# Fetching norm weight rows two norms ahead, and summing two halves of an attention output in one operation, in a two-block transformer kernel

## The reference, cut to what matters

```python
def group_layernorm(x, g):                 # used for each gMLP group and each retention head
    mu = mean(x); var = mean((x - mu)**2)
    return (x - mu) * rsqrt(var + EPS) * g # g: 128 weights for each group or head

outs.append(einsum('bhqk,bkhe->bqhe', attn, vb))   # both attentions: probabilities times values
```

## Time and profile before

| what | value |
|---|---|
| median of 3 runs | 4096.31 us (4092.6 to 4104.3) |
| profiled execution, its own time | 4091.48 us |
| span of its trace | 4089.7 us |
| busy PE, DVE, ACT, POOL | 3780.2, 2004.9, 1698.1, 798.5 us |
| mean TensorE clock granted | 0.964 of full |
| data moved | 774.97 MB, mean 189 GB/s |

### The profile page before, as it was taken

How to read it: one execution, slowest core, us unless ns; L and a number is a source line. 1 busy time by engine, 2 the same in 40 slices (tenths; PEclk the granted TensorE clock), 3 DMA queues, 4 the chain that set the end, 5 groups by cost and what they waited for, 6 DMA issues and landing times.

```text
span 4089.7 us, 59374 instructions
## 1 busy us (share of the span) xinstructions
PE 3780.2 (92%) x23304; PEld 3384.3 (83%) x23304; DVE 2004.9 (49%) x4355; ACT 1698.1 (42%) x3455; POOL 798.5 (20%) x704
## 2 busy tenths in 40 slices
PE   7989899999998889999999989999988999999897
PEld 6878788877778789888879988888878989888897
DVE  4446565546656555555545545445566543111433
ACT  4334455546654444455533334334554533111322
POOL 3434333444443321100011000110000000001000
PEclk9999999999999999999999999999999999999999
DMA  6886666776665557545454445454453345555343
GB/s 184 266 267 188 181 200 246 247 250 236 239 222 184 190 189 261 180 164 185 156 184 137 169 167 201 175 181 162 155 180 111 134 162 215 185 187 206 140 157 138
DMA packets 331815, 774.97 MB, mean 189 GB/s; under 512 B 36241, under 2 KB 220561, under 8 KB 275218
## 3 DMA queue, kind: packets, MB, share of 16 engines
q1 hardware_dynamic: 270482, 731.31, 51.5%
q10 hardware_dynamic: 61056, 39.86, 3.5%
HBM read 591.49 MB, written 179.59 MB: 189 GB/s over the span
## 4 chain that ended last, share of the span: by engine, by line
PE 50%; DVE 9%; ACT 3%; issue 2%; DMA 2%; SPq 0%; POOL 0%; DVEq 0%; ACTq 0%
PE PS L1267 13%; PE PS L1269 13%; PE PS L1268 13%; PE PS L1372 2%; PE PS L1358 2%; DMA GROW<-in_gmlp_ln_g 2%; PE PS L1350 1%; PE PS L1349 1%; PE PS L1374 1%; DVE PT L1892 1%; DVE PP L1923 1%; DVE SM L1860 1%; PE PS L1328 0%; DVE BIG L1791 0%; SPq L2382 0%
## 5 line engine op out<-in xcount | busy, mean ns | idle before, releaser
L1267 PE MATMUL PS<-WF,BIG 128*128 128x256 f32 x2768 | 813.6, 294 | 55.2 <-DVE BIG L1783 16.7
L1268 PE MATMUL PS<-WF,BIG 128*128 128x256 f32 x2768 | 799.1, 289 | 0.0
L1269 PE MATMUL PS<-WF,BIG 128*128 128x256 f32 x2768 | 798.4, 288 | 0.0
L1267 PE MATMUL PS<-BIG,WF 128*128 128x512 f32 (+1 forms) x1792 | 693.1, 387 | 9.5 <-POOL WF L2158 4.6
L1269 PE MATMUL PS<-BIG,WF 128*128 128x512 f32 (+1 forms) x1792 | 680.0, 379 | 0.0
L1268 PE MATMUL PS<-BIG,WF 128*128 128x512 f32 (+1 forms) x1792 | 679.1, 379 | 0.0
L2158 POOL TENSOR_TENSOR WF<-RAW,WF 128x512 fp32r<-128x512 f32 x380 | 504.5, 1350 | 804.4 <-ACT WF L1472 804.3
L1267 PEld LDWEIGHTS PS<-WF,BIG 128*128 128x128 f32 x2768 | 546.0, 197 | 70.3 <-issue 15.9
L1268 PEld LDWEIGHTS PS<-WF,BIG 128*128 128x128 f32 x2768 | 546.3, 197 | 7.9 <-issue 2.3
L1269 PEld LDWEIGHTS PS<-WF,BIG 128*128 128x128 f32 x2768 | 545.7, 197 | 0.0
L1892 DVE TENSOR_TENSOR PT<-PS,PT 128x512 fp32r<-128x512 f32 (+3 forms) x320 | 195.0, 609 | 596.4 <-ACT PT L1587 595.7
(11 more groups left out here) (222 smaller groups left out, 6858.4 us busy)
## 6 DMA issues: line engine op xcount, KB each, us to landing
WF<-scratch_WS SPq DMA_DIRECT2D x264, 1024.0 KB, 5.1
scratch_WS<-WF SPq DMA_DIRECT2D x110, 1024.0 KB, 6.4
W<-scratch_WS SPq DMA_DIRECT2D x66, 1024.0 KB, 5.0
RAW<-in_w_in SPq DMA_DIRECT2D x84, 512.0 KB, 4.5
KV<-scratch_KS SPq DMA_DIRECT2D x60, 512.0 KB, 5.6
KV<-scratch_VS SPq DMA_DIRECT2D x60, 512.0 KB, 5.2
QQ<-scratch_QS SPq DMA_DIRECT2D x192, 128.0 KB, 5.0
XH<-in_x SPq DMA_DIRECT2D x32, 512.0 KB, 6.0
```

The lines of the kernel that those rows point to most:

```text
L1267: pe.matmul(o, Ah, Bh, start=first, stop=False)
L1268: pe.matmul(o, Ah, Bl, start=False, stop=False)
L1269: return pe.matmul(o, Al, Bh, start=False, stop=last)
```

## The change

The order of all 32 rows is written out ahead. The first two rows are asked for at the start of the first chunk's second block. Behind every norm the row of the norm two places further is asked for, set aside until 4 units of projection cost have passed; this crosses from one chunk to the next. The place in GROW, and the norm that the request waits for (the one just computed), are as the ring of two gives them. `take_out` becomes one tensor_reduce that adds the two parts.

```diff
+        grow = Ring(2)
+        row_of = {}
+        rows_to_come = deque()
+        for c in range(NC):
+            for kind, i, _ in mix_units():
+                rows_to_come.extend([("ret", c, i, ("rn", c, i))] if kind == "r" else [("gmlp", c, 2 * i + gi, ("gv", c, 2 * i + gi)) for gi in range(2)])
+
+        def ask_row(us=0):
+
+            if rows_to_come:
+                tag, at_c, i, read = rows_to_come.popleft()
+                row_of[tag, at_c, i], before = grow.take(read)
+                step = ("load_grow", tag, at_c, i, row_of[tag, at_c, i], before)
+                after(us, step) if us else do(step)
...
-            grow = Ring(2)
...
-            def take_row(which, g, read):
-                row, before = grow.take(read)
-                do(("load_grow", which, c, g, row, before))
-                return row
+            if c == 0:
+                ask_row()
+                ask_row()
...
             def gmlp_norm(p, gi, buf, tok):
                 g = 2 * p + gi
-                row = take_row("gmlp", g, ("gv", c, g))
-
                 def norm():
                     do(("gmlp_stats", c, g, buf, tok))
                     rstd("proj", ("gm", c, g), 4, 4, 1.0, [("ag", "gmlp", c, g)], "mv")
-                    do(("gmlp_norm", c, g, buf, row))
+                    do(("gmlp_norm", c, g, buf, row_of["gmlp", c, g]))
                     used_rstd["proj"].append(("gv", c, g))
+                    ask_row(4)
                 return norm
...
-                row = take_row("ret", h, ("rn", c, h))
-
...
-                    do(("ret_norm", c, h, bufs, row, yb_after))
+                    do(("ret_norm", c, h, bufs, row_of["ret", c, h], yb_after))
                     used_rstd["proj"].append(("rn", c, h))
+                    ask_row(4)
                     store(("ry", c, h), 512 + 128 * h)
...
-                dve.tensor_copy(dst, src[:, :, 0, :]).then_inc(*inc("o_step", ("o1", c, j, qt)))
-                on.wait_ge("o1", c, j, qt)
-                dve.tensor_tensor(dst, src[:, :, 1, :], dst, ALU.add).then_inc(*inc("o_step", ("o2", c, j, qt)))
+                dve.tensor_reduce(dst, src.rearrange("p r a e -> p r e a"), AX, ALU.add).then_inc(*inc("o_step", ("o2", c, j, qt)))
```

## The result

The changed kernel takes 4038.11 us at the median of four runs (4034.3 to 4038.55), against 4094.45 us of the kernel before beside it (4092.51 to 4104.3). The ratio is 0.9856, with a 95% interval from 0.9838 to 0.9873: 56 us off, where 40 were forecast. The span of the profiled execution goes from 4089.7 to 4036.7 us. The direction and the kind of gain were right; the size was not, and the forecast's base of 4096.31 us scaled by the ratio gives 4037.3, just under the range's lower end of 4038.

The account below looks back on a forecast made before the run. PE was taken as the bound, busy 92% of the span, with only some 310 us of idle time to be had. Rows 36, clock 7 and output 2 made 45 us, less 5 gives 40: median 4056 us, range 4038 to 4079.

Parts of the forecast that it names:

- Part 1, the rows: DVE's waits for rows at gMLP norms: all 56.4 us go, giving 36.5 us of PE idle time.
- Part 2, the clock: PE's lower clock behind long gaps: four windows at 1.8 us go, 7 us; bounds 0 and 13.
- one for each chunk: Four low-clock windows of 4 us taken as gone, at each chunk's last norm or its like, 1.8 us each.
- the eleven smaller waits: DVE row waits other than the chunks' last norms: 27.7 us, paired to 17.9 us of PE idle time.
- The 5 us taken off at the end: Taken from the sum of 45 us for gaps where another releaser stands close behind the one removed.
- The smaller-of-two pairing: For each row wait, the smaller of DVE's wait and the PE gap following it counts as PE's gain.
- Part 4, the output: take_out's reduce at 424 ns against 573 saves 14 us of DVE, 2 us of time; ends 14 and -9.
- Part 3, SP: Requests on SP's queue: SP may stand about a microsecond behind a gMLP norm; cost put at 0.
- Half of it coming back: Rival: PE meets table changes, copied results or splitting at nearly the same instant; gain 18 us, median 4078; chance 0.14.
- Rows staying late: Rival: SP reaches the request as late as the old one; gain under 12 us, 4090; chance 0.07.
- Slower through SP: Rival: loads behind the request in SP's queue go out late; costs 60 us, giving 4116; chance 0.05.

Follow-up runs that it names:

- run 3: Kernel before, with only g3's row (last norm of each chunk) asked for early, behind g2's norm: 4073.88 us, ratio 0.9951.
- run 4: Changed kernel, but with g3's row asked for where it was before, behind the eight copies: 4063.86 us, ratio 0.9930.
- full_again: Changed kernel measured once more, five rounds on one chip beside the kernel before (4101.32 us): 4038.8 us, ratio 0.9847.
- run 2: Kernel before with one tensor_reduce in take_out and the old row requests: 4092.23 us over ten runs, ratio 0.9990.
- run 1: Changed kernel with the old copy and add in take_out, so only the rows moved: 4047.66 us, ratio 0.9894.
- Run 11: Changed kernel with 116 useless PE transposes in seven gaps and 24 in each of two gaps ahead of copied results: 4033.5 us, ratio 0.9850.
- Run 7: Changed kernel with the reduce of take_out carried out three times, each waiting for the one before: 4077.94 us, 39 us above full_again.
- runs 5 and 6: Side by side on one chip: full_again, 4038.8 us, and the changed kernel with the old copy and add in take_out, 4043.59 us, ratio 0.9864.
- run 9: Changed kernel with each row request directly behind its norm instead of 4 units of cost later: 4041.96 us, ratio 0.9877.
- run 10: Changed kernel with each row request 10 units of cost behind its norm instead of 4: 4047.98 us, ratio 0.9887.

## Why the prediction was right in kind and short in size

**Part 1, the rows: held.** 56.4 us of DVE's waiting were to go, and went. 36.5 us of PE's idle time were to go; 35.0 went with the rows alone, 38.8 with both parts. By halves, 18.6 and 17.9 were forecast, and runs 3 and 4 show 15.6 and 18.0 (the latter with the output's part in it). PE's waits for the norm's product went from 15.6 us in 8 to 4.3 in 5.

**Part 2, the clock: the step that failed.** The prediction took one window of 4 us at half clock for each chunk, 7 us, with 13 as its bound. The clock share lost in and behind the four stretches fell from 33.8 to 16.8 us: 17 us. In PE's busy time it was 14.2 us, and 17.5 in full_again's profile. Where it came back is seen when the windows from 4 us ahead of each last norm to 30 us behind it are taken apart from the rest of the stretches:

| kernel | around the four last norms | rest of the stretches |
|---|---|---|
| before | 12.4 | 21.4 |
| output's sum alone (run 2) | 11.8 | 20.9 |
| last rows early (run 3) | 4.2 | 19.8 |
| all rows early but the last (run 4) | 10.0 | 10.9 |
| rows alone (run 1) | 4.6 | 12.7 |
| full change | 6.2 | 10.6 |
| full_again | 4.7 | 10.9 |

Around the last norms 6 to 9 us came back, where the prediction had 7: that part was sized right in sum, though not "one for each chunk". Chunk 0 gave more than one window (4.2 to 1.5), since a second gap followed there and the low clock came twice. Chunk 1 gave next to nothing (1.8 to 1.7), since the 3.47 us that are left of its gap are again followed by a window at 0.57; the prediction had this as its lower bound:

```profile
2372.00:2376.00 4.00, 4.00 (x20) 3.75 (x19) 2.15 (x5) 1.04 (x3) 0.00 (x0) 0.57 0.00 0
```

The step that failed is the other one: the clock behind the eleven smaller waits was put at nothing in the sum, and at 6 us in the bound of 13. It gave back 9 to 11 us, in every kernel that moved those eleven rows, and not in runs 2 and 3, which did not (0.6 and 1.6). With one profile each, a microsecond or two of it can be chance. Run 11 shows, with the release of PE left where it was, that a gap of this size costs by the clock behind it.

**The 5 us taken off at the end: wrong.** They stood for another releaser close behind the one removed. The smaller-of-two pairing had already left that part out, gap by gap. What is left behind the norms is what the pairing had left standing: 3.47 us in chunk 1, where it said 3.2, and the gaps for the copied results in chunks 0 and 3, 3.4 and 3.3, which were there before (2.8 and 3.6). So the deduction counted it twice. Only run 3, with 15.6 us for 18.6, shows something of what it stood for.

**Part 4, the output: right duration, price too low.** The reduce took 415 ns; 424 was forecast. That reads set its time fits the other reduces of the same profile, which read 128, 256, 384 and 512 elements to one result and take 292, 425, 558 and 684 ns. The Trainium skill's warning on tensor_reduce ("VectorE: DVE Perf Modes", "Rules for kernel authors") does not hold for this use: one reduce of 256 elements took 415 ns, the copy and the add that it replaces 573. But the 2 us counted only PE gaps that the profile puts down to the output itself. Run 7 gives 0.48 us for each microsecond of DVE time there, so 7 us, and runs 5 and 6 give 4.8; run 2, with the rows still late, gave 4 with an interval from nothing to 9. A likely reason, not isolated by a run, is that the operations behind it on DVE (maxima, splits) are late by the same time, and their waits carry other names.

**Part 3, SP: right that it costs nothing, for a weaker reason than stated.** SP stands 3.2 us at a gMLP request on average (41.7 in 13), not about one. PE's waits for weights, queries and copied results stayed where they were. Behind retention norms the prediction's reason held: in run 9 the 88 us at the request took the place of 93 at the store behind it (101.3 less 8.5).

**Sum after the fact.** In PE's own times the gain of the span is 38.8 idle + 14.2 busy = 53.0 us in the first profile and 40.9 + 17.5 = 58.4 in full_again's, with the output's part in both terms. Against the forecast's 40 the clock was short by 7 to 10 us, the deduction took 5 too many, and the output was short by 3 to 5: 15 to 20 us, where the two sets of runs have 16 and 22 more than forecast. The 36.5 of idle time for the rows is the term that was right.

**The rivals.** Half of it coming back: out as a whole, though it happened in chunk 3, where some 5 us of the stretch's gain came back behind the last norm. Rows staying late: out as the change stands, but run 10 shows it begin when the request is put off from 4 to 10 units, in chunk 0 first. Slower through SP: out by the result itself, and by PE's waits for loads, which did not grow; run 9 adds little, since its standing is mostly moved and not new.

## What to carry to other kernels

When a small load holds up an engine in program order, pair each of its waits with the gap that follows on the engine that sets the end and take the smaller number. That gave the idle time to within a few microseconds here and needs no further deduction. Then price the clock by itself: add up, window by window, the busy time spent below full clock in and behind the gaps that will go, small ones included; where a gap is only shortened (10.02 to 3.47 us in chunk 1) the low clock can stay. For an operation on a busy in-order engine, the waits that bear its own name are a floor; its delay is passed on under the names of what stands behind it.

## What the runs showed of the hardware that was not expected

- Idle gaps cost PE their length and then slow matmuls. Behind the gap of 3.05 us shown above the granted clock was 0.63 over 4 us, while with 23 useless transposes in the gap it stayed at 1.00. A gap of 2.25 us in the kernel before was followed by a window at 1.00, while one of 2.05 us at 1500.6 us, just behind the window at 0.51, was followed by one at 0.66: the length of the gap alone does not tell. The transposes cost 0.12 us each and paid for themselves.
- A tensor_reduce that adds pairs lying 64 or 128 elements apart in PSUM, with 128 results, took 415 ns, no more than the 424 ns of a reduce of 256 neighbouring elements to one result.
- The same copy of one row lands in 6.0 us at the median where it is asked for in a burst, 3.9 where it is moved 4 units behind its norm, and 3.0 in the run that asks at once. It is back at 5.8 in run 10, which asks 10 units behind. What sets it was not isolated.
- The first 1290 us of the kernel, which the rows' part leaves alone, took 1292 to 1299 us in the four profiled kernels with the old output operations, and 1284 to 1291 in those with one reduce. The means, 1295 and 1288, differ by 7 us, which fits the price of run 7, since that part of the kernel holds much of the attention. Of a change worth a few microseconds, only the stretches that it touches can tell it from that.
